# Layer step with 32 routed experts on one core: expert rounds 0 to 2 from the strips of experts 0 to 3, rounds 0 and 1 ahead of the last tile's routing

## The reference

```python
x = x + m @ w_out
xn = rmsnorm(x, ln2_g)
g_idx = argmax(xn @ w_rg + b_rg)            # 1 of 4 groups
top_v, top_i = top_k(softmax(le_sel), 2)    # 2 of the 8 experts of the group
hh = silu(xn @ wg[e]) * (xn @ wu[e]) * comb # per chosen expert, 1024 -> 256
y += hh @ wd[e]                             # 256 -> 1024
out = rmsnorm(x + y, final_g)
```

## Time and profile before

| what | us |
|---|---|
| median of 3 runs (792.17 to 797.22) | 795.99 |
| span of the profiled execution, first to last instruction | 778.5 |
| difference, what lies around the span | 17.5 |
| PE busy (94% of the span) | 730.6 |
| DVE busy | 410.1 |
| POOL busy | 212.0 |
| DMA, mean over the span | 227 GB/s |

### The profile page before, as it was taken

One profiled execution on the slowest core, in us unless ns is written; L12 is line 12 of the kernel. 1 busy time (PEld: TensorE's weight loads), 2 busy tenths in 40 slices (PEclk: granted clock), 3 DMA queues, 4 the chain that ended last, 5 costly groups with the idle time before them and its releaser, 6 DMA issues.

```text
span 778.5 us, 11578 instructions
## 1 busy us (share of the span) xinstructions
PE 730.6 (94%) x4361; PEld 354.9 (46%) x4361; DVE 410.1 (53%) x1121; ACT 218.0 (28%) x512; POOL 212.0 (27%) x246
## 2 busy tenths in 40 slices
PE   9999999899999999999999479999999999999485
PEld 6555556566666655555655322232222322233131
DVE  0776677765875854866664753233332333221366
ACT  3565646413362363211111101111111111101132
POOL 1011111010231233111211274554445544411111
PEclk9999999999999999999999679999999999999887
DMA  8911030130110016873214969999999999998196
GB/s 318 336 56 42 28 124 1 28 142 5 58 61 0 1 55 235 309 274 122 96 54 166 376 223 379 408 417 412 419 412 415 415 416 416 416 408 351 55 387 241
DMA packets 36506, 176.68 MB, mean 227 GB/s; under 512 B 8164, under 2 KB 14492, under 8 KB 26186
## 3 DMA queue, kind: packets, MB, share of 16 engines
q1 hardware_dynamic: 27058, 157.36, 51.3%
q0 software_dynamic: 8960, 17.24, 5.9%
q10 hardware_dynamic: 432, 1.34, 0.4%
HBM read 158.93 MB, written 27.35 MB: 239 GB/s over the span
## 4 chain that ended last, share of the span: by engine, by line
PE 73%; DVE 12%; ACT 5%; DMA 5%; issue 4%; SPq 1%; POOL 0%; DVEq 0%; POOLq 0%; ACTq 0%
PE PS L2079 22%; PE PS L2095 11%; PE PS L1908 6%; PE PS L1900 6%; PE PS L1886 4%; PE PS L1736 4%; PE PS L1867 3%; DMA BIG<-ypair 2%; PE PS L1737 2%; PE PS L1856 2%; DVE RD L1155 2%; PE PS L1720 2%; PE PS L1948 1%; DMA cst<-in_cst 1%; PE PS L2116 1%
## 5 line engine op out<-in xcount | busy, mean ns | idle before, releaser
L2079 PE MATMUL PS<-BIG,RD 128*32 128x512 f32 x1536 | 171.8, 599 | 2.4 <-issue 1.6
L817 POOL DMA_INDIRECT RD<-xtab,rot x92 | 93.3, 1014 | 28.1 <-issue 28.1
L2079 PEld LDWEIGHTS PS<-BIG,RD 128*32 128x32 f32 x1536 | 48.4, 111 | 108.4 <-issue 108.4
L2095 PE MATMUL PS<-BIG,RD 128*32 128x512 f32 x672 | 86.8, 592 | 0.0
L1622 DVE SCALAR_TENSOR_TENSOR RD<-RD,PS 128x256 f32<-128x256 f32 x25 | 10.5, 421 | 127.8 <-ACT RD L1075 127.8
L1736 PE MATMUL PS<-BIG 128*128 128x512 f32 x128 | 66.1, 598 | 0.7 <-DMA BIG<-in_wqkv 0.7
L716 POOL TENSOR_TENSOR stat<-stat,mhalf 128x1 f32<-128x1 f32 (+1 forms) x27 | 15.5, 575 | 186.3 <-DVE stat L1145 84.0
L1900 PE MATMUL PS<-BIG 128*128 128x512 f32 x128 | 61.1, 624 | 0.0
L841 POOL DMA_INDIRECT ypair<-RD,pids x25 | 25.7, 1027 | 130.0 <-DVE RD L1638 108.2
L1908 PE MATMUL PS<-BIG 128*128 128x512 f32 x128 | 57.8, 595 | 0.2 <-DVE xin L1418 0.2
L1886 PE MATMUL PS<-BIG 128*128 128x344 f32 x192 | 57.3, 454 | 0.0
(11 more groups left out here) (307 smaller groups left out, 1059.2 us busy)
## 6 DMA issues: line engine op xcount, KB each, us to landing
BIG<-in_wexp SPq DMA_DIRECT2D x33, 2048.0 KB, 21.1
BIG<-in_wexp SPq DMA_DIRECT2D x29, 1024.0 KB, 23.0
BIG<-ypair SPq DMA_DIRECT2D x8, 1024.0 KB, 11.0
xin<-in_x SPq DMA_DIRECT2D x13, 512.0 KB, 3.7
BIG<-in_wxy SPq DMA_DIRECT2D x4, 1024.0 KB, 4.8
xin<-in_wexp SPq DMA_DIRECT2D x4, 1024.0 KB
BIG<-x2d SPq DMA_DIRECT2D x1, 4096.0 KB
out_y<-RD SPq DMA_DIRECT2D x8, 512.0 KB, 5.5
```

The costliest lines, as they stand in the source:

```text
L817: pool.indirect_dma_start(xg[:, p3, j * CHUNK_D:(j + 1) * CHUNK_D], None, xtab.rearrange("t (q e) -> (t q) e", q=NQ), bass.IndirectOffsetO ...
L2079: o = MM(PS[own, 2 + p2, :], xgT[:, p2, at:at + STRIP], wgu[expert(n, j) % NG][:, k * 512:(k + 1) * 512], start=(k == 0), stop=(k == KD - 1))
L2095: o = MM(PS[own, 5 + half, :], hT[:, p2, k, own], wdn[expert(n, j) % ND][:, at:at + 512], start=(k == 0), stop=(k == KF - 1))
```

## The change

1. A strip's round is new for experts 0 to 3 (`NEARLY`): round s (0, 1, 2) holds strip s of experts 0, 1, 2, 3. From round 3 on the order is the old one. So `last_round` of experts 0, 1, 2 and 3 is 2 for all.
2. Round 0 may hold tokens of steps 0 to 5 only, round 1 those of steps 0 to 6. `room` lifts the counts of experts 0 to 3 to 32, then to 64, so that later tokens go to later strips. Two small list transposes on PE (`early_lists`), the row numbers on DVE (`early_rows`), and POOL's `gather(0)` ahead of `scatter(6)`, `gather(1)` behind `root2` of the last tile.
3. DVE waits for `gather(0)` and does `turn(0)` between `position(6)` and `x2_half(8, 0)`.
4. PE does gate-up of round 0 in three pieces between `ranks(7)`, `turn_x2(8, 1)`, `router(8)` and the lists; `hT(0)` and half of y(0) stand ahead of `add_lists(8)`, the rest behind it, then gu(1), gu(2), y(1).
5. The row gather, PE transposes and ACT copies of round 0 go.
6. Slot lists hold 2 times the token row plus 0 or 1, so the numbers for `spread` come from DVE (`pids_all`) and the list in DRAM is read in round 6, for the overflow unit alone. `overflow_table` moves from ahead of round 0 into round 3.
7. `xtab` and `ypair` are laid out with the decode tokens first (`ROW`); `lev`, `bigc`, `hh`, `hT` move to other memory, and PSUM banks of the rounds change.
8. Buffers 2, 3 and 4, 5 of gate-up change places. SP loads gate-up 2 and 3 early; gate-up 4 behind down 1 and 2; gate-up 5 and down 4 only when the last tile's `xtab` write has landed. The load for the overflow unit waits one round longer, the `x2d` load no longer waits for `gu_ps`.

```diff
+NEARLY = PER_R
+NFIRST = NEARLY * PER_E
-F_G, F_D = (NE - NG) % NG, (NE - ND) % ND
+F_G, F_D = (NE - NG + 2) % NG, (NE - ND) % ND
...
+        def strip_of(e, s):
+            return NEARLY * s + e if e < NEARLY else PER_E * e + s
         def expert(r, j):
-            return (PER_R * r + j) // PER_E
+            i = PER_R * r + j
+            return j if i < NFIRST else i // PER_E
         def last_round(e):
-            return (PER_E * e + PER_E - 1) // PER_R
+            return strip_of(e, PER_E - 1) // PER_R
...
                 if i in (1, 2):
-                    load_gu(i + 3)
+                    load_gu(i + 1)
             sp.wait_ge(xT2_ps, 2 * (NT - 1))
-            load_gu(2)
             load_dn(1)
             load_dn(2)
+            load_gu(4)
             sp.wait_ge(op_ps, 2 * NT)
-            load_gu(3)
             load_dn(3)
+            sp.wait_ge(xt_out[(NT - 1) % 2], 16 * ((NT + 1) // 2))
+            load_gu(5)
             load_dn(4)
...
                 root2(i)
+                if i == NT - 2:
+                    pool.wait_ge(pid_ok, 1)
+                    for p in range(2):
+                        pool.wait_ge(xt_out[p], 16 * 3)
+                    gather(0)
                 scatter(i - 1)
...
             root2(NT - 1)
+            pool.wait_ge(pid_ok, 2)
...
+            gather(1)
             scatter(NT - 2)
...
+            pool.wait_ge(pid_ok, 3)
+            pool.wait_ge(xt_out[0], 16 * 5)
+            gather(2)
...
                 x2_half(i, 1)
+                if i == NT - 2:
+                    dve.wait_ge(kwin_out, 64)
+                    early_rows(0)
                 variance2(i)
                 norm2(i)
+                if i == NT - 2:
+                    room(0)
                 place(i - 1)
                 position(i - 1)
+                if i == NT - 2:
+                    turn(0)
                 x2_half(i + 1, 0)
                 choose(i)
             x2_half(NT - 1, 1)
+            room(1)
+            place(NT - 2)
+            early_rows(1)
             weights(NT - 2)
+            variance2(NT - 1)
...
+            unit_h(unit(0))
             place(NT - 1)
...
+            addresses(2 * NEARLY, NSTRIP, 2, NU)
+            turn(1)
             position(NT - 1)
             weights(NT - 1)
+            unit_y(unit(0))
             turn(2)
+            unit_h(unit(1))
+            turn(3)
...
+            ranks(NT - 2)
+            early_lists(1)
+            round_gu(unit(0), range(0, 2))
+            turn_x2(NT - 1, 1)
+            round_gu(unit(0), range(2, 5))
+            router(NT - 1)
+            round_gu(unit(0), range(5, KD))
+            lists_start()
             add_lists(NT - 2)
             ranks(NT - 1)
+            unit_hT(unit(0))
+            round_y(unit(0), range(1))
             add_lists(NT - 1)
+            round_y(unit(0), range(1, 2))
+            round_gu(unit(1), range(KD))
```

More of the change, by code:

```diff
@@ L63 @@
 MAXV = TOPK * TOKENS // (SLOTS + 1) + 1
+NEARLY = PER_R
+ROW = [NDEC + t * P for t in range(NPT)] + [0]
+SEEN = [ROW[TURN[NT - 3]], ROW[TURN[NT - 2]], TOKENS]
+NFIRST = NEARLY * PER_E
 NG = 6
@@ L254, in build @@
         x2t = RD.cut(512)
+        RD.phase(5 * D_MODEL)
         lg = RD.cut(8)
@@ L803, in _ @@
             root2(NT - 1)
+            pool.wait_ge(pid_ok, 2)
+            pool.wait_ge(xt_out[0], 16 * 4)
+            pool.wait_ge(xt_out[1], 16 * 4)
+            gather(1)
             scatter(NT - 2)
[L805 to L820, removed]
+            pool.wait_ge(pid_ok, 3)
+            pool.wait_ge(xt_out[0], 16 * 5)
+            gather(2)
             def gather_rows(v, col):
@@ new lines, in room, with addresses @@
+            def room(n):
+                V.tensor_scalar(cnt[:, 0:NEARLY], cnt[:, 0:NEARLY], float(STRIP * (n + 1)), None, ALU.max).then_inc(dve_done, dq.up())
+                dve.wait_ge(dve_done, dq.now())
+            def addresses(lo, hi, r0, r1):
+                dve.wait_ge(dve_done, dq.now())
+                V.tensor_scalar(tokn[:, lo:hi], pair[:, lo:hi], 1, None, ALU.logical_shift_right).then_inc(dve_done, dq.up())
+                dve.wait_ge(dve_done, dq.now())
+                V.tensor_scalar(pid[:, lo:hi], tokn[:, lo:hi], float(NQ), cst[:, K_Q:K_Q + 1], ALU.mult, ALU.add).then_inc(pid_ok, 1)
+                for j in range(PER_R):
+                    own = slice(STRIP * j, STRIP * j + STRIP)
+                    o = V.tensor_copy(pids_all[own, r0:r1], pair[own, lo + j:hi:PER_R])
+                o.then_inc(pair_ok, 1)
@@ new lines, in early_rows, with turn @@
+            def early_rows(n):
+                dve.wait_ge(el_ps, n + 1 + EL_PS)
+                lo = PER_R * n
+                V.tensor_scalar(pair[:, lo:lo + PER_R], PS[:, EL_BANK[n], 3 * NE:3 * NE + NEARLY], 2.0 * TOK0, None, ALU.add)\
+                    .then_inc(dve_done, dq.up())
+                addresses(lo, lo + PER_R, n, n + 1)
+            def turn(n):
+                dve.wait_ge(xg_in[n % 3], 16 * PER_R * (n // 3 + 1))
+                if n >= 2:
+                    dve.wait_ge(gu_ps, n - 1)
+                V.transpose(xgT[n % 2], xg[n % 3].rearrange("p (j c k) -> p j k c", j=PER_R, k=KD)).then_inc(xgd_ok, 1)
@@ L1571, in _ @@
             V.tensor_copy(xT2[:, 4:8, :], PS[:, t_bank(NT - 1, 1), :].rearrange("q (a c) -> q a c", a=4)).then_inc(xT2d_ok, 1)
-            place(NT - 2, between=lambda: variance2(NT - 1))
             sums(NT - 2)
@@ L1653, in _ @@
+            for n in range(1, NU):
                 unit_h(unit(n + 1))
@@ L1658, in _ @@
                     turn(n + 3)
+                if n == 3:
+                    overflow_table()
             unit_y(unit(NU))
@@ L1967, in spread_lists, with early_lists @@
                 return PS[STRIP * q:STRIP * q + STRIP, 1 + s, 0:NE]
+            def early_lists(n):
+                pe.wait_ge(held_ok, NT - 3 + n)
+                for q in range(NQ):
+                    o = MM(PS[STRIP * q:STRIP * q + STRIP, EL_BANK[n], 3 * NE:3 * NE + NEARLY],
+                           ident[0:SLOTS, STRIP * n:STRIP * n + STRIP], held[0:SLOTS, 0:NEARLY], start=True, stop=True)
+                o.then_inc(el_ps, 1)
             pe.wait_ge(xl_ok, 3 * NFT + 1)
@@ L2072, in round_gu @@
                     pe.wait_ge(xgd_ok, n + 1)
-                for k in range(KD):
-                    if (n, k) == (1, 4):
-                        unit_hT(unit(0))
+                for k in ks:
+                    if (n, k) == (2, 4):
+                        unit_hT(unit(1))
                     for j in range(PER_R):
@@ L2147, in _ @@
                     unit_x(unit(NU))
-                round_y(unit(n))
+                round_y(unit(n), range(2))
                 unit_hT(unit(n + 1))
```

345 lines of the change are left out of this document (174 added, 171 removed).

## The result

The changed kernel took 810.4 us (804.1 to 813.1, four executions) against 794.4 us (792.2 to 797.2) for the kernel before: ratio 1.0194, 95% interval 1.0145 to 1.0243. I had forecast 803 (788 to 811), with 0.47 for a time within 1% of the kernel before and 0.38 for a slower one. The time lies in the range by 0.6 us, and it is the second of these, not the first, that came. In the executions of the experiments both kernels are 10 to 15 us shorter, 784.9 and 795.3 us, and the ratio is 1.0172 (1.0108 to 1.0237). The change costs 10 to 16 us, where my forecast had 7.

What follows compares the result with a forecast made beforehand. The weight stream, not PE, was taken to bind: expert 29 lands at 688.2 against 681.4, +6.8 us. 778.5 + 6.8 = 785.3 span, plus 17.5 around it, 802.8; likewise against the median; forecast 803, range 788 to 811.

Steps and rivals of the forecast that it cites:

- T: End of gu(2), round 2's gate-up, in the changed kernel; gate-up 6 cannot be issued before; forecast 473.2 us, 468 to 477.
- T + 215.0: Landing of expert 29's gate-up load, needed by round 21: 88.8 MB take 214.0 us, plus 1.0 until data flow; 688.2.
- first rival: Rounds on PE, not the weight stream, were the limit: 788 us, at best 783; chance 0.16.
- overflow of the rooms: Rival: slots wasted by `room` push a second expert beyond 96, adding a whole unit, over 11 us: 815; chance 0.01.
- t0: Reference time in each profile: first load of the block that waits for the transposes of the next-to-last tile.
- a): DVE waits for `gather(0)` ahead of `x2_half(8, 0)`, which starts at 429.3 instead of 424.9: +4.4 us, bounds +0.3 and +4.9.
- b): PE idles some 4 us during DVE's wait; a half-projection partly at half clock loses 0 to 1.7 us, taken as 0.8.
- c) to f): Early row and room operations +1.3 us, `unit_h(0)` +0.9, `hT(0)` and half of y(0) +1.1, two list-to-row-number steps +0.5.
- PE's lead: PE begins gu(3) at 477.1 instead of 485.3, 8 us ahead, then uses this up waiting for weights in later rounds.
- The waits cost clock: Rival: PE waiting for weights in late rounds loses clock, two to four us on top: 806 to 809; chance 0.20.
- Gather 0 lands early: Rival: gather 0 lands early and PE's clock stays up, stream 2 to 4 us late: 798 to 799; chance 0.24.

Runs made afterwards that it cites:

- b_late: Kernel before with one SP wait added: no load of gate-up 6 or later before gate-up of round 2 has ended; 796.1 us, ratio 1.0165.
- a_half: Changed kernel with half of each gate-up load from expert 6 on left out; 783.0 us, ratio 0.9977 to the kernel before.
- a_again: Changed kernel once more, unchanged; 795.3 us, ratio 1.0172 to the kernel before.
- a_hold: Changed kernel with SP waiting for gather(2) to land before issuing gate-up 5 and down 4, 5 and 6; 799.0 us, ratio 1.0213 to the kernel before.
- b_again: Kernel before once more, unchanged, for a second profile; 783.6 us, ratio 0.9992.
- b_more: Kernel before with three small indirect gathers more, in rounds 12, 14 and 16, into a tile nobody reads; 779.6 us, ratio 0.9941.

## Why the prediction was right, and where it was off

**The stream (right).** That the kernel before was bound by its weights and not by PE, that experts 0 to 3 give back their buffers only at T, that PE's head start is spent in waits ahead of every third round: all this stood, and T + 215.0 was 214.2 to 214.9 in six of the seven profiles that kept both this order and its loads. `b_late` shows it alone. The first rival (rounds were the limit) is refuted by it and by `a_half`. The overflow of the rooms did not occur.

**T (too early, the step that failed).** I had T = t0 + 51.8, it was 58.7. By my steps, from t0, in `a_again`:

- a) x2_half(8, 0) at 9.2 for a forecast of 7.9. The gather's fourth issue began at 0.3 instead of -0.4 (the first of the four took 1.92 us instead of 1.0), and DVE took the rows up 6.95 us after it, where I had 6.2 (a landing of 6.7 in the earlier trace rows). The upper bound of 4.9 us was passed: the shift was 5.7. The wait was named right, its size was too small, and what it did to b) was too.
- b) PE idle for 5.3 us, then the half-projection of the earlier trace rows in 5.84 us, at a granted clock of 0.50 and 0.70: 2.2 us, beyond my 1.7 at worst, where I took 0.8.
- c) to f) Row numbers ready at 35.4, forecast 33.1: of the 2.3 more, 1.3 came from a) and 1.4 from b), so that the four small steps together were sized right, within half a microsecond.
- From there to the last issue of gather(2) 4.9 us instead of 3.9: POOL waits for the address copies too and starts 0.9 us after the row numbers stand. I had left them out.
- The rows usable 6.9 us after that issue instead of 5.2. Beside the loads issued from 453 to 456 it is the 6.5 of the earlier trace rows again; my discount was not earned. `a_hold` shows that the loads are its cause.
- The turn, the start of PE and gu(2) 11.5 us instead of 9.6: PE had been idle for 4.0 us,

```profile
core 0: us, PE busy (x), PEclk, DMA share, GB/s
434.40:437.80 3.40, 3.40 (x8) 0.50 0.24 101
437.80:441.00 3.20, 3.20 (x8) 0.70 0.00 0
473.50:477.00 3.50, 3.50 (x24) 0.55 0.28 79
...
587.50:591.50 4.00, 4.00 (x20) 0.50 1.04 423
660.50:664.50 4.00, 4.00 (x24) 0.63 1.02 416
```

and the first half of gu(2) took 5.34 us where a whole one takes 7.07. The third of these lines is that stretch, the first two are step b)'s, and the last two the first 4 us of the gate-ups of rounds 12 and 18: I had charged the clock once, at step b), though gu(2) starts behind a wait of 4.0 us. Behind each of the four waits of 3.9 us and more that PE has in `a_again` between t0 and round 21 the work is drawn out (the half-projection of 5.84 us, the half gate-up of 5.34, the gate-ups of 9.95 and 8.77), at a granted clock of 0.50 to 0.63 at first. Behind shorter waits it goes either way: after 2.09 us a gate-up takes 8.77 in `b_late`, after 2.30 us 7.07 in `a_hold`. The Trainium skill, TensorE: Matmul & The Clock Gate, on oscillation, has the clock fall again in each wait for DMA; the trace agrees for the long waits.

**The end (two errors that cancel in part).** With T at 58.7 my own formula gives + 13.7 us over the kernel before (16.7 from t0, less 3.0), and round 21 starts 11.4 us later from t0 than in `b_again`, 12.8 later than in the earlier trace rows. From there on I forecast no difference. The pair rows came 2.0 us sooner (9.62 for 11.57), and the closing drain added 5.1. From `b_again` to `a_again` the whole account is: t0 earlier by 1.3, T later by 16.0, the stream quicker from there by 4.5, pair rows - 2.0, the rest of the last part - 2.1 (1.5 of it a shorter second wait for pair rows), drain + 5.1: 11.2, which is 793.8 - 782.6. Without the drain, which I could not have read from any row, the change costs 5 us by the medians and 7.4 from t0 on in these two profiles; so the forecast of 7 was too small for two reasons, T too early by 6.9 us and the drain missing, and too large by what the last part gained.

That the time itself lay within 788 to 811 is in part luck. The profiled execution at 813.1 is outside, 12 us of it the slow issue that no term of mine had, and the set was about 10 us longer for the kernel before as well. The ratio is the fairer measure: 1.009 forecast, 1.019 there and 1.017 in the second set.

**PE's lead (too large).** I had PE 8 us ahead at gu(3). It started at t0 + 62.4, against 64.6 in `b_again`, 2.2 us ahead, since T was 6.9 us later than I had it. It made no difference to the end.

**The rivals.** "The waits cost clock" had the mechanism right (rounds of 9.95 and 8.77 us), and its price is inside T + 214: it is paid while PE waits for the stream anyway. "Gather 0 lands early", which was what the rule on queues in the Trainium skill's DMA: Bandwidth & Descriptors gave, did not happen: DVE took up the rows 6.95 us after the last issue. The measurement decides.

## What to carry to other kernels

Before work is moved forward into a hole, ask which buffers it holds and whose load waits for them: where a stream of weights is full to the end, the time at which its first buffer comes free sets the end, and filling an engine's idle hole in front of it was worth nothing here. One added wait on the loads, in an otherwise unchanged kernel, is the cheap experiment that tells this. And when loads are held back to speed up something small, count the idle time of the DMAs that it makes against it.

## What the runs showed of the hardware that I had not expected

POOL's closing drain is a cost of its own, 1.53 us (kernel before), 3.97 (`b_more`) or 9.53 to 9.77 (all with the change), which the chain doesn't show. With the change, neither 64 more instructions, nor three indirect DMAs fewer, nor a POOL copy in each round changed it by more than 0.3 us. With three small indirect DMAs more (and two waits with them) in the kernel before, POOL stands 2.5 us less in front of its last spread, where it is on the path, and drains 2.4 us longer, where it is covered: 779.6 us against 783.6, the only version with full loads here that beats both kernels.

PE can issue at less than a fifth of its rate for 18 us (13 matmuls in 7.76 us) at a granted clock of 1.00 with hardly anything to wait for in the profile; it was seen in one of the nine profiles with this order of the lists, where it put T 12 us later. Its cause is open.
